# A mixture-of-experts router computed tile by tile, with the norm's weight folded into its matrix and its bias logits made one mixer earlier

## The reference

```python
for l in range(2):
    mix = hybrid_mixer(x, ...)
    x = layer_norm(DN_ALPHA * x + mix, ln1_w[l], ln1_b[l])
    if l == 0:
        f = swiglu_2(x, ffn_w_gate, ffn_w_up, ffn_w_down)
    else:
        f = moe_swiglu(x, moe_router, moe_w_gate, moe_w_up, moe_w_down)
    x = layer_norm(DN_ALPHA * x + f, ln2_w[l], ln2_b[l])

def moe_swiglu(x, router, wg, wu, wd):
    t = x.reshape(256, 1024)
    logits = t @ router                       # router is 1024 x 8
    top_v, top_i = lax.top_k(logits, 2)
    top_w = jax.nn.softmax(top_v, axis=-1)
    gate = (one_hot(top_i, 8) * top_w[..., None]).sum(1)
    y = 0
    for e in range(8):
        y = y + gate[:, e:e + 1] * swiglu_2(t, wg[e], wu[e], wd[e])
    return y
```

## Time and profile before

| | us |
|---|---|
| median of 3 runs | 2725.54 (2724.69 to 2726.2) |
| the profiled execution's own time | 2725.77 |
| its span in the trace | 2723.7 |
| PE busy | 2662.9 (98%) |
| DVE busy | 1201.7 (44%) |
| ACT busy | 355.9 (13%) |
| experts, from the first product L1859 on | starts at 1830.28 |

### The profile page before, as it was taken

One profiled execution on the slowest core, in us unless ns is written; L12 is line 12 of the kernel. 1 busy time (PEld: TensorE's weight loads), 2 busy tenths in 40 slices (PEclk: granted clock), 3 DMA queues, 4 the chain that ended last, 5 costly groups with the idle time before them and its releaser, 6 DMA issues.

```text
span 2723.7 us, 84033 instructions
## 1 busy us (share of the span) xinstructions
PE 2662.9 (98%) x39442; PEld 2178.0 (80%) x39442; DVE 1201.7 (44%) x1925; ACT 355.9 (13%) x730; POOL 18.5 (1%) x28
## 2 busy tenths in 40 slices
PE   8999998999999999999999999999999999999997
PEld 5789666697599466994657965659999999999997
DVE  2678864487688524885357763450000000000011
ACT  2210123100100012000241000420000101000000
POOL 1000000000000000000000000000000000000000
PEclk9999999999999999999999999999999999999999
DMA  7345412655445532645325544349999999999994
GB/s 206 124 156 163 163 63 94 209 178 178 149 158 172 185 124 78 195 148 185 115 101 166 162 172 162 105 155 399 411 410 402 398 412 393 409 399 396 409 399 194
DMA packets 269230, 619.50 MB, mean 227 GB/s; under 512 B 10326, under 2 KB 128348, under 8 KB 256636
## 3 DMA queue, kind: packets, MB, share of 16 engines
q1 hardware_dynamic: 266064, 606.14, 60.3%
q0 software_dynamic: 2400, 10.09, 1.3%
q10 hardware_dynamic: 588, 0.63, 0.1%
HBM read 615.77 MB, written 1.05 MB: 226 GB/s over the span
## 4 chain that ended last, share of the span: by engine, by line
PE 95%; DVE 3%; ACT 1%; issue 0%; DMA 0%; SPq 0%; DVEq 0%; ACTq 0%
PE ps L1186 25%; PE ps L1859 20%; PE ps L1874 10%; PE ps L1238 10%; PE ps L1077 8%; PE ps L1088 7%; PE ps L1274 3%; PE ps L1368 2%; PE ps L1791 2%; PE ps L1846 1%; PE ps L1826 1%; PE ps L1477 1%; PE ps L1579 0%; PE ps L1350 0%; DMA ring<-in_fox_w_in 0%
## 5 line engine op out<-in xcount | busy, mean ns | idle before, releaser
L1859 PE MATMUL ps<-arena,ring 128*64 128x88 f32 x14336 | 550.2, 239 | 2.3 <-issue 2.3
L1859 PEld LDWEIGHTS ps<-arena,ring 128*64 128x64 f32 x14336 | 545.9, 138 | 3.6 <-issue 3.4
L2816 DVE TENSOR_TENSOR arena<-arena,ps 128x352 f32<-128x352 f32 x64 | 30.4, 476 | 706.5 <-PE ps L1859 706.5
L1077 PE MATMUL ps<-xT,ring 128*128 128x256 f32 (+2 forms) x960 | 213.0, 381 | 3.2 <-DVE arena L2245 0.9
L1186 PE MATMUL ps<-arena 128*64 128x128 f32 x3520 | 211.6, 273 | 0.0
L1077 PEld LDWEIGHTS ps<-xT,ring 128*128 128x128 f32 (+2 forms) x960 | 177.0, 186 | 36.8 <-issue 8.8
L1186 PE MATMUL ps<-xT,ring 128*64 128x128 f32 x3520 | 202.6, 273 | 0.0
L1186 PE MATMUL ps<-arena,ring 128*64 128x128 f32 x3520 | 201.9, 273 | 0.0
L1186 PEld LDWEIGHTS ps<-arena 128*64 128x64 f32 x3520 | 196.7, 137 | 0.0
L1186 PEld LDWEIGHTS ps<-xT,ring 128*64 128x64 f32 x3520 | 193.9, 137 | 3.2 <-issue 2.8
L1186 PEld LDWEIGHTS ps<-arena,ring 128*64 128x64 f32 x3520 | 194.4, 137 | 0.0
(11 more groups left out here) (477 smaller groups left out, 2821.2 us busy)
## 6 DMA issues: line engine op xcount, KB each, us to landing
ring<-in_moe_w_gate SPq DMA_DIRECT2D x64, 1792.0 KB, 11.1
ring<-in_moe_w_up SPq DMA_DIRECT2D x64, 1792.0 KB, 11.4
ring<-in_moe_w_down SPq DMA_DIRECT2D x32, 2048.0 KB, 11.9
ring<-in_ffn_w_gate_up SPq DMA_DIRECT2D x44, 1024.0 KB, 5.2
ring<-in_ffn_w_gate_up SPq DMA_DIRECT2D x88, 512.0 KB, 7.1
arena<-in_moe_w_down SPq DMA_DIRECT2D x32, 1024.0 KB, 10.1
ring<-in_ffn_w_down SPq DMA_DIRECT2D x55, 512.0 KB, 6.6
ring<-in_ffn_w_down SPq DMA_DIRECT2D x25, 1024.0 KB, 5.0
```

The costliest lines, as they stand in the source:

```text
L1077: ins = pe.matmul(o, lhsT=w[:, k, c0:c0 + m], rhs=rhs[:, k, :], start=(k == 0), stop=(k == kt - 1))
L1859: ins = pe.matmul(ps[h, bank, c0:c0 + CAP], lhsT=w_f[:, k, h], rhs=xe[:, 4 * kh + k, :], start=(kh == k == c0 == 0), stop=(kh == 1 and k = ...
L2816: dve.tensor_tensor(hid_e[:, c0 * CAP:(c0 + n) * CAP], silu_e[:, c0 * CAP:(c0 + n) * CAP], ps[:, bank, 0:n * CAP], ALU.mult).then_inc(hid_ ...
```

## The change

At the second hybrid layer's entry PE makes the bias logits `b @ R` into bank 7 (eight products whose stationary operand is a column of the norm's bias spread over 128 tokens, L1158 of the changed kernel). They stand ahead of the keep-warm products there, which become two instead of four ahead of tile 0. All keep-warm products of this call go to bank 6, since bank 7 is taken. DVE copies the bias logits to `router_b` ahead of its copies to `xT`.

Within that layer, ahead of the mixer's output additions, DVE multiplies the router by the norm's weight into `router_w`.

Ahead of the router, `turn_z(4)` is replaced by `turn_tile`. Each tile is turned into two banks of its own, and each bank is copied without scaling by one instruction of 128x512: three on ACT, one on DVE. The logits are products of 128 tokens against `router_w`, four feature groups at a time: tile 0's first half ahead of tile 1's transposes, the rest behind them. The two keep-warm products between the tiles are gone, and the two behind the logits stay. DVE adds `router_b` as it reads the logits, and finds the best two of tile 0 before it waits for tile 1.

```diff
@@ -392,6 +392,8 @@
         y_e = cv(D)
         route = cv(10, TT, N_EXP)
         router = small[:, 128:192]
+        router_w = arena[:, 26368:26368 + KD * N_EXP]
+        router_b = arena[:, 26368 + KD * N_EXP:26368 + (KD + 1) * N_EXP]
         route_idx = sb("route_idx", [P, TT, N_EXP], U32)
         overflow = sb("overflow", [P, 1], I32)
         N_ST = F_EXP // EW
@@ -463,6 +465,7 @@
         rows_loaded = sem("row_vectors_loaded")
         rows_used = sem("row_vectors_used")
         overflow_ready = sem("overflow_flag_ready")
+        route_scaled = sem("router_scaled")
         router_loaded = sem("router_loaded")
         late_step = sem("dve_late_step_done")
         late_to_act = sem("last_variance_for_act")
@@ -811,8 +814,8 @@
                             act.activation(small[:, 4 + i:5 + i], small[:, 38 + i:39 + i], ACT.Sqrt, scale=1.0 / D,
                                            bias=small[:, 36 + i:37 + i]).then_inc(act_to_dve, 1)
 
-            def ln_scale():
-                for i in range(TT):
+            def ln_scale(tiles=range(TT)):
+                for i in tiles:
                     act.wait_ge(dve_to_act, t.up("dve_to_act"))
                     act.activation(small[:, 4 + i:5 + i], small[:, 61 + 2 * i:62 + 2 * i], ACT.Sqrt, bias=eps2)\
                        .then_inc(act_to_dve, 1)
@@ -917,7 +920,16 @@
             ln_scale()
             turned_z(0, "ln2_w_2", "ln2_b_2", 0)
             hybrid(1)
-            ln_scale()
+
+            def keep_turned(i, h):
+                full()
+                drain(act.activation(xT[:, 4 * h:4 * h + 4, i * P:(i + 1) * P],
+                                     ps[:, 4 + 2 * i + h, :].rearrange("p (k n) -> p k n", n=P), ACT.Copy))
+            ln_scale((0,))
+            keep_turned(0, 0)
+            ln_scale((1,))
+            keep_turned(0, 1)
+            keep_turned(1, 0)
             def moe_pass():
                 def xe_copy(ks=range(KD)):
                     for k in ks:
@@ -960,7 +972,6 @@
                 gate_T_copy()
                 y_rows_copy()
 
-            turned_z(4, "ln1_w_2", "ln1_b_2", 1)
             act.wait_ge(dve_to_act, t.up("dve_to_act"))
             act.activation(route[:, 9, :, 0:1], route[:, 9, :, 0:1], ACT.Exp).then_inc(act_to_dve, 1)
             moe_pass()
@@ -1135,12 +1146,20 @@
                 return to_dve(pe.matmul(ps[:, b, 0:S], lhsT=cst("ones"), rhs=r_diag[:, :, :].rearrange("p i n -> p (i n)"),
                                         start=True, stop=True), b)
 
-            def turn_z(base):
+            def turn_z(base, route=False):
 
                 tks = []
                 for i in range(TT):
+                    if route and i == 0:
+                        pe.wait_ge(router_loaded, 16)
+                        claim(7)
+                        for k in range(KD):
+                            b = NORM_AT["ln1_b_2"] + KD + k
+                            ins = pe.matmul(ps[:, 7, 0:N_EXP], lhsT=norm_vec[:, b:b + 1].to_broadcast([P, P]),
+                                            rhs=router[:, k * N_EXP:(k + 1) * N_EXP], start=(k == 0), stop=(k == KD - 1))
+                        to_dve(ins, 7)
                     if base == 0 or i == 1:
-                        keep_warm((1 if base == 0 else 2) if i else 4, 7 - base)
+                        keep_warm((1 if base == 0 else 2) if i else 2 if route else 4, 6 if route else 7 - base)
                     pe.wait_ge(z_ready, t.up("z_ready"))
                     for j in range(4):
                         claim(base + j)
@@ -1814,7 +1833,7 @@
             tks = [tk for _, tk in turn_z(4)]
             keep_warm(1, 3)
             ffn(tks[0:2], tks[2:4], (), plain=False)
-            hybrid(1, turn_z(0))
+            hybrid(1, turn_z(0, route=True))
             def moe_pass(nth):
 
                 def gather(n, halves=False):
@@ -1943,18 +1962,35 @@
                 for b in range(8):
                     holder[b] = (drained_dve, t.value("drained_dve"))
 
-            waits = turn_z(4)
-            pe.wait_ge(router_loaded, 16)
-            for i in range(TT):
-                claim(i)
-                for k in range(KD):
-                    for first, tk in waits if i == 0 else ():
-                        if k == first:
-                            pe.wait_ge(*tk)
-                    for h in HALVES:
-                        ins = pe.matmul(ps[h, i, 0:N_EXP], lhsT=xT[:, k, i * P + h.start:i * P + h.stop],
-                                        rhs=router[:, k * N_EXP:(k + 1) * N_EXP], start=(k == 0), stop=(k == KD - 1))
-                to_dve(ins, i)
+            pe.wait_ge(route_scaled, 1)
+            claim(0, 1)
+            turned = []
+
+            def turn_tile(i):
+                pe.wait_ge(z_ready, t.up("z_ready"))
+                for h in range(2):
+                    b = 4 + 2 * i + h
+                    claim(b)
+                    for kk in range(4):
+                        k = 4 * h + kk
+                        ins = pe.transpose(ps[:, b, kk * P:(kk + 1) * P], x[:, i, k * P:(k + 1) * P], ident)
+                        if k == i == 0:
+                            carry(ins)
+                    turned.append((to_dve if i == h == 1 else to_act)(ins, b))
+
+            def logits(i, h):
+                pe.wait_ge(*turned[2 * i + h])
+                for k in range(4 * h, 4 * h + 4):
+                    ins = pe.matmul(ps[:, i, 0:N_EXP], lhsT=xT[:, k, i * P:(i + 1) * P],
+                                    rhs=router_w[:, k * N_EXP:(k + 1) * N_EXP], start=(k == 0), stop=(k == KD - 1))
+                if h == 1:
+                    to_dve(ins, i)
+            turn_tile(0)
+            logits(0, 0)
+            turn_tile(1)
+            logits(0, 1)
+            for h in range(2):
+                logits(1, h)
             keep_warm(2, 3)
             pe.wait_ge(dve_to_pe, t.up("dve_to_pe"))
             sel = route[:, 5]
@@ -2586,8 +2622,6 @@
                     dve.wait_ge(act_to_dve, t.up("act_to_dve"))
                     token_sums(early=True)
                     token_sums(early=False)
-                if ver == 13:
-                    return
                 dve.wait_ge(rows_loaded, t.up("rows_loaded", 32 if b else 16))
                 wide = rowv[:, 0, :].unsqueeze(1).to_broadcast([P, TT, D])
                 ins = dve.tensor_tensor(x[:, :, :], x[:, :, :], wide, ALU.mult)
@@ -2744,7 +2778,13 @@
                 tt(h0, h0, r_g, ALU.mult).then_inc(dve_to_pe, 1)
                 if l == 0:
                     weight_sums(0, 3)
-                mix_out(alpha=DN_ALPHA)
+                    mix_out(alpha=DN_ALPHA)
+                else:
+                    dve.wait_ge(router_loaded, 16)
+                    a = NORM_AT["ln1_w_2"] + KD
+                    tt(router_w.rearrange("p (k e) -> p k e", e=N_EXP), router.rearrange("p (k e) -> p k e", e=N_EXP),
+                       norm_vec[:, a:a + KD].unsqueeze(2).to_broadcast([P, KD, N_EXP]), ALU.mult).then_inc(route_scaled, 1)
+                    mix_out(alpha=DN_ALPHA)
 
             def drain_and(ins):
                 dve.wait_ge(drained_dve, drain(ins))
@@ -2754,6 +2794,8 @@
             hybrid(0)
             turned_z(4, "ln1_w_2", "ln1_b_2", 0, 11, sums=True)
             ffn(3, alpha=DN_ALPHA)
+            full()
+            drain(dve.tensor_copy(router_b, ps[:, 7, 0:N_EXP]))
             turned_z(0, "ln2_w_2", "ln2_b_2", 0, 12)
             hybrid(1)
             def moe_pass(b):
@@ -2849,14 +2891,18 @@
                 dve.wait_ge(overflow_ready, 1)
                 return dve.value_load(overflow[0:1, 0:1], min_val=0, max_val=1)
 
-            turned_z(4, "ln1_w_2", "ln1_b_2", 1, 13)
             lg, mx, ixf, oh1, oh2, sel, gate, posm, wgt, dif = (route[:, i] for i in range(10))
-            for i in range(TT):
+
+            full()
+            drain(dve.tensor_copy(xT[:, 4:8, P:S], ps[:, 7, :].rearrange("p (k n) -> p k n", n=P)))
+
+            def best(i):
                 full()
-                drain_and(dve.tensor_copy(lg[:, i, :], ps[:, i, 0:N_EXP]))
-            for i in range(TT):
+                drain_and(dve.tensor_tensor(lg[:, i, :], ps[:, i, 0:N_EXP], router_b, ALU.add))
                 then(dve.max(mx[:, i, :], lg[:, i, :]))
                 then(dve.max_index(route_idx[:, i, :], mx[:, i, :], lg[:, i, :]))
+            for i in range(TT):
+                best(i)
             dve.tensor_copy(ixf, route_idx[:, :, :])
             then(dve.memset(dif, 0.0))
             dve.tensor_tensor(dif[:, :, 0:1], mx[:, :, 1:2], mx[:, :, 0:1], ALU.subtract).then_inc(dve_to_act, 1)
```

## The result

The changed kernel takes 2729.54 us (median of 19 runs, 2727.71 to 2732.77), the kernel before 2724.42 us (19 runs, 2721.47 to 2726.2). The ratio is 1.002 with a 95% interval of 1.0013 to 1.0026, so +5.1 us, at the edge of what I had called no change. The forecast was +4.2 us, 2729.7 us in all. The total came out closer than the change did: the forecast started from 2725.54 us, the median of three runs, which is 1.1 us above the median of 19, and its change is 0.9 us too small.

A forecast was written before the change was run, and what follows sets the result against it. PE, holding 95% of the chain of waits, was taken to bound the kernel. 2725.77 + 2.8 (entry) + 1.4 (router) = 2730.0 us profiled, so 2729.7 us forecast; range 2725.8 to 2732.9.

The forecast's parts named there:

- The wait for bank 6: Second hybrid layer's entry: keep-warm products wait for DVE's last addition from bank 6, delaying the transposes, +1.1 us.
- The half clock at the entry: Second hybrid layer's entry: narrow records and waiting make the clock fall, slowing keep-warm products, +1.7 us.
- bound of +3.0: Entry's upper limit for half clock: two keep-warm products +1.7, the transposes and third keep-warm product +1.3.
- The router: Router: logits and keep-warm products slowed by half clock, +1.4 us, bounds -1.6 to +3.2.
- the fall: Router: granted clock drops to half between 1814.6 and 1817.3, taken as 1816.3.
- The places: Router: places start behind the keep-warm products at 1823.3, 2.2 us later than before.
- the clock that was back by then: Router: full clock from the places to the first gather saves 0.8 us.
- a clock that holds: Router without half clock: selection and places 0.8 us earlier, first gather another 0.8 us sooner, -1.6 us.
- What was forecast as free: Entry and mixer: DVE's bias-logit copy and router multiplication cost nothing, 0.2 us each if uncovered; bias logits' time already covered.
- The clock held: Rival: no half clock at entry or router, 1.1 - 1.6 = -0.5 us, 2725.0 us; chance 0.10.
- The long half clock: Rival: half clock outlasts the keep-warm products at entry and router, +7.3 us, 2732.8 us; chance 0.18.
- The stall in the first expert stretch: Rival: PE's 1.72 us stall in the experts' first loop moves, -1.7 to +1.7 on the forecast; chance 0.10.

The follow-up runs named there:

- the repeat: The changed kernel measured once more, unedited: +4.1 us against the kernel before, ratio 1.0016.
- all three: Changed kernel with keep-warm products in bank 7 ahead of the bias logits, keep-warm products around tile 0's first logits, and logits split in halves: -2.5 and -0.6 us against before.
- router keep-warm: Changed kernel plus one keep-warm product (bank 3) on either side of tile 0's first four logit products: +2.3 us against before, ratio 1.0008.
- part 1 alone: Kernel before with only the changed entry of the second hybrid layer (bias logits, keep-warm products in bank 6), old router: +3.1 us against before, ratio 1.0011.
- bank 7 first: Changed kernel with tile 0's two keep-warm products put in bank 7 ahead of the bias logits: +3.6 us against before, ratio 1.0010.
- part 2 alone: Changed kernel with the old hybrid entry, bias logits left out and router_b set to zero: +4.1 us against before, ratio 1.0012.

## Why the prediction was right

- **The wait for bank 6.** Forecast +1.1 us at full clock, measured 9.10 - 7.94 = +1.16. The wait stood where it was read from the code and the earlier trace rows, released by the addition behind tile 0's scaling. The narrow products were sized right too: 16 records took 1.85 us, forecast 1.9.
- **The half clock at the entry.** Forecast +1.7, measured 1.7 in the first trace (10.79 against 9.10), 1.5 to 1.6 in three others, 3.1 in the repeat. My bound of +3.0 had a slip: eight transposes (0.87 us) and a keep-warm product (0.86) at half clock add 1.7, not 1.3, so it should have been +3.4, and the repeat stays below that. The places of both falls in the earlier trace rows, behind a stretch of narrow records and waiting, were a good enough guide to this one. The Trainium skill ("TensorE: Matmul & The Clock Gate", Part 4: PE-mode transpose), by which a transpose does not hold the clock up, agrees with the falls at the router (0.50 from 1817.3 in the changed kernel). It says nothing of the fall at the entry, which had no transpose in front of it, and no run tests it alone: at 1810.00 to 1826.60 of all three the clock stayed at 1.00 with the same transposes in place, once products of 512 columns stood between them.
- **The router.** Forecast +1.4, measured +1.1 in the first pair of traces and +1.8 over the means. Its inner terms: the fall came at about 1817.2, 4.8 us behind the first transpose, forecast 5.2; 24 records at mixed clock took 4.5 us, forecast 2.8 + 1.8 = 4.6; the keep-warm products 3.3, forecast 3.4. The places came 1.9 us later, forecast 2.2, and the clock that was back by then gave 0.75 us, forecast 0.8. With a clock that holds the forecast was -1.6; router keep-warm has 17.66 against 19.13, -1.5. But 0.8 of that is the half clock of before, which the old router does without in part 1 alone; against a full clock the gain is 0.7 us. The forecast took the half clock of before for a fixed part of the old router, and that is not so.
- **What was forecast as free was free**: the copy of the bias logits runs behind the scaling of tile 1, the bias logits take the place of two keep-warm products (bank 7 first, 7.94). The mixer, with the multiplication of the router in it, took 147.86 to 148.18 us wherever its own half clock was as short as before, against 148.06.
- **The rivals.** The clock held in no trace of the entry with its wait unfilled, and in none of the unrepaired router. The long half clock came at one place at a time, 6.8 us in the repeat's entry and 10 us in the router of bank 7 first, and in no trace at both. The stall in the first expert stretch moved (0.25 us in the up products and 2.9 in two waits in the down products, against 2.3 before), +0.8 us where the experts' stretch is +0.7; that it is instruction loading was not tested.
- **The range.** "Each part within half of its bounds" gives 2727.4 to 2731.3 and not 2727.5 to 2731.9. The forecast and the range that was stated do not hang on it.
- **What was luck.** That the total is off by 0.2 us only: a start 1.1 us too high and a change 0.9 us too small nearly cancel. The sum of the changed stretches is 3.9 us in the first pair of traces, and the remaining 0.9 us of 4.8 is unchanged code at a changed clock, a mixer of +1.1 and an end of +1.8 against a beginning of -2.7. The last scatter shows it plainly, first before and then after:

```profile
2704.80:2708.50 3.70, 3.69 (x8) 1.42 (x8) 2.48 (x4) 1.21 (x1) 0.00 (x0) 1.00 0.03 9
```

```profile
2707.80:2715.00 7.20, 6.97 (x8) 2.31 (x8) 4.33 (x7) 1.28 (x1) 0.00 (x0) 0.51 0.03 7
```

Taken over all traces the two places come to 11.0 - 7.9 = 3.0 us for the entry (five traces with its wait and its quiet time, 10.6 to 12.2) and 1.8 us for the router, 4.8 in all. That agrees with the medians of +5.1 and +4.1. The half clock under the last scatter is in five of the 14 traces, part 1 alone and part 2 alone among them, and not in the changed kernel's repeat, so it belongs to neither part; what decides where it falls is open.

## What to carry to other kernels

A filler product needs a place to write, and the bank it is given decides what it waits for: before moving one, look up who reads that bank last, and what stands behind the filler in the queue. Filler products between waits can pay for what comes behind them (router 17.66 and 18.86 us with them, 20.2 to 21.8 without), so a shorter path that takes them out has to be priced at half clock; put them where nothing has to wait for them. When an edit is worth a few microseconds, cut the trace at fixed records and compare the stretches, since unchanged code moved by 1 to 4 us from one execution to the next. And look whether the old kernel's own trace holds a half clock at the place: it can be gone in its next execution, and then it is no gain of the change.

## What the runs showed of the hardware

- A product with a 128x128 float32 stationary operand and 8 columns costs 0.11 us a record at full clock (24 records in 2.74 us), one with a 128x64 operand 0.033 us (48 in 1.57 us). So the 128 tokens of a tile are quicker in two halves, 0.066 us, than in one full record, 0.11.
- The granted clock fell in the same code in one execution and not in another (the old router 19.13 and 18.33 us; with the keep-warm products between the tiles 17.66, and 18.86 with the same ones in another kernel), so the price of a quiet stretch is a range, here 0 to 3 us, and not a number.
